# mLSTM units of a one-step diffusion backbone: decay-maximum rows spread by transfers, scaled keys in two buffers, the carried part scaled by ScalarE, PSUM banks laid out anew

## The reference, cut to what matters

```python
b = jnp.cumsum(fb, axis=-1)
log_d = jnp.where(causal, b[..., :, None] - b[..., None, :] + ib[..., None, :], -jnp.inf)
inter = b + m[..., None]
m_t = jnp.maximum(inter, jnp.max(log_d, axis=-1))
s = jnp.einsum('bhtd,bhsd->bhts', qb, kb) * jnp.exp(log_d - m_t[..., None])
w_inter = jnp.exp(inter - m_t)
num = w_inter[..., None] * jnp.einsum('bhtd,bhde->bhte', qb, C) + jnp.einsum('bhts,bhse->bhte', s, vb)
den = w_inter * jnp.einsum('bhtd,bhd->bht', qb, n) + jnp.sum(s, axis=-1)
h = num / jnp.maximum(jnp.abs(den), jnp.exp(-m_t))[..., None]
...
C_new = decay[..., None, None] * C + jnp.einsum('bhs,bhsd,bhse->bhde', w_s, kb, vb)
n_new = decay[..., None] * n + jnp.einsum('bhs,bhsd->bhd', w_s, kb)
```

## Time and profile before

| | us |
|---|---|
| median of 3 runs (lowest, highest) | 2070.65 (2065.98, 2072.45) |
| the profiled execution's own time | 2071.18 |
| its span | 2069.4 |
| PE busy | 1908.4 (92%) |
| DVE busy | 1238.8 (60%) |
| ACT busy | 1086.9 (53%) |
| POOL busy | 706.1 (34%) |

### The profile page before, as it was taken

The page is one execution under the profiler, slowest core; times in us unless marked ns, Lnnn a source line. Parts: engine busy times, 40 slices in busy tenths (PEclk is TensorE's granted clock), DMA queues, the critical chain, the costliest instruction groups (busy, mean ns, idle before and its releaser), DMA issues.

```text
span 2069.4 us, 31383 instructions
## 1 busy us (share of the span) xinstructions
PE 1908.4 (92%) x8796; PEld 1332.9 (64%) x8797; DVE 1238.8 (60%) x1754; ACT 1086.9 (53%) x1548; POOL 706.1 (34%) x738
## 2 busy tenths in 40 slices
PE   8879998999998996799999999999999999999980
PEld 3434445999886454566777767767777777776750
DVE  3575437333777588775666666555566665555646
ACT  5435455342234333565666666666666666665652
POOL 2211000000023044544445534345666653434431
PEclk9999999999999998899999999999999999999995
DMA  8742101342005224347957997866688788886875
GB/s 295 257 143 83 42 21 41 122 123 61 1 1 179 92 92 173 123 158 239 332 169 230 314 343 245 292 186 169 179 263 260 242 272 271 311 296 228 305 198 189
DMA packets 118443, 390.10 MB, mean 189 GB/s; under 512 B 27817, under 2 KB 52461, under 8 KB 93421
## 3 DMA queue, kind: packets, MB, share of 16 engines
q1 hardware_dynamic: 74348, 276.95, 36.2%
q0 software_dynamic: 43744, 112.34, 21.4%
q10 hardware_dynamic: 290, 0.02, 0.0%
HBM read 346.03 MB, written 79.88 MB: 206 GB/s over the span
## 4 chain that ended last, share of the span: by engine, by line
PE 25%; DMA 25%; issue 4%; DVE 3%; ACT 1%; POOL 1%; POOLq 1%; DVEq 0%; ACTq 0%; SPq 0%
DMA yacc_scratch<-y,idx_s 24%; PE bank L1986 14%; PE bank L2009 9%; PE bank L1973 2%; POOL slot_table L1923 1%; DVE wupl L2162 1%; DMA xg<-hn_scratch,idx_g 1%; DVE big L2255 1%; PE bank L1993 1%; DVE xTl L2171 0%; DVE big L2247 0%; DVE y L2246 0%; ACT wuph L2086 0%; DMA shared<-slot_table 0%; DMA y<-yacc_scratch 0%
## 5 line engine op out<-in xcount | busy, mean ns | idle before, releaser
L2162 DVE TENSOR_TENSOR wupl<-big,wuph 128x2048 fp32r<-128x2048 f32 x230 | 517.0, 2289 | 451.0 <-ACT wuph L2086 395.7
L2086 ACT ACTIVATE wuph<-big 128x2048 fp32r (+1 forms) x230 | 428.4, 1916 | 12.5 <-issue 8.5
L2009 PE MATMUL bank<-w,hT 128*128 (+1 forms) x912 | 412.0, 595 | 1.4 <-ACT hT L2071 1.4
L1986 PE MATMUL bank<-wuph,xTh 128*128 128x512 f32 x912 | 367.2, 403 | 12.2 <-DVE xTl L2171 11.9
L1915 POOL DMA_INDIRECT yacc_scratch<-y,idx_s x105 | 220.2, 2097 | 429.4 <-issue 392.8
L1986 PE MATMUL bank<-wuph,xTl 128*128 128x512 f32 x912 | 359.3, 394 | 0.0
L1986 PE MATMUL bank<-wupl,xTh 128*128 128x512 f32 x912 | 358.3, 393 | 0.0
L2009 PEld LDWEIGHTS bank<-w,hT 128*128 128x128 f32 x912 | 165.3, 191 | 166.1 <-issue 166.1
L2076 ACT ACTIVATE y<-bank 128x512 f32<-128x512 f32 x114 | 68.1, 597 | 281.7 <-PE bank L2009 247.6
L1986 PEld LDWEIGHTS bank<-wuph,xTh 128*128 128x128 f32 x912 | 173.4, 190 | 48.5 <-issue 9.7
L1986 PEld LDWEIGHTS bank<-wuph,xTl 128*128 128x128 f32 x912 | 172.2, 189 | 36.7
(11 more groups left out here) (355 smaller groups left out, 2691.9 us busy)
## 6 DMA issues: line engine op xcount, KB each, us to landing
big<-in_exp_w SPq DMA_DIRECT2D x128, 1024.0 KB
w<-in_exp_w SPq DMA_DIRECT2D x64, 1024.0 KB, 7.5
wada<-in_w_ada POOLq DMA_DIRECT2D x16, 1024.0 KB, 6.3
wg<-in_w_in SPq DMA_DIRECT2D x14, 1024.0 KB, 5.3
wada<-in_w_ada SPq DMA_DIRECT2D x4, 2048.0 KB, 19.1
big<-in_w_in SPq DMA_DIRECT2D x8, 1024.0 KB, 5.3
x<-x_scratch SPq DMA_DIRECT2D x9, 512.0 KB
x_scratch<-x SPq DMA_DIRECT2D x9, 512.0 KB, 2.6
```

The costliest lines, as they stand in the source:

```text
L1986: mm = pe.matmul(b_up[j][:, :], x[:, k, :], w[:, :, k, :], start=(k == 0 and i == 0), stop=(k == KT - 1 and i == 2))
L2009: mm = pe.matmul(b_down[half][:, :], hT[:, i, :], w2[:, at, i, half * 512:(half + 1) * 512].rearrange("p s n -> p (s n)"), start=(i == 0), ...
L2086: act.activation(part13(wup[j][0], half), raw13(e % WSLOT, half), ACT.Copy).then_inc(w_high, 1)
L2162: dve.tensor_tensor(part13(wup[j][1], half), raw13(e % WSLOT, half), part13(wup[j][0], half).bitcast(F32), ALU.subtract).then_inc(w_low, 1)
```

## The change

- In the RG-LRU stage SP writes the rows `m.mn` to DRAM once (`mn_rows`). In the mLSTM stage POOL loads, for each unit, the four heads' rows of 128 floats to all 128 partitions (`spread_rows`, 256 KB from repeated rows of 512 bytes), into one of four buffers; the first four before the units, the others four units ahead, behind POOL's inverse root. PE's product L1135 and its bank PM are gone. DVE's L1354 reads the buffer in SBUF and waits for its transfer; the wait for the scores stands before L1359 now.
- `kw` has two buffers, so L1280 of unit n + 1 waits for `products` of unit n - 1.
- The scaling L1365 is done by ACT, behind L1280 of unit n + 1, and signals `carried`. DVE updates S first, then waits for `carried`, then adds; `unit_done` comes after the additions. PE's second half of the first output projection waits for `carried`, since it writes a bank that ACT reads.
- The products of a unit lie in five banks instead of four: those with the state in banks 3 and 4, the weighted scores' in 5 and 6, the increments in 6 and 7.
- Several semaphores are merged (`m.cleared`, `m.squared`, `m.rooted`), with the counts adapted in the other stages.

```diff
             sp.wait_ge(row_d, 4)
             sp.dma_start(o[4][0, 0].rearrange("d h -> h d"), mfin[:, :], allow_slow_non_contiguous=True).then_inc(s_out, 16)
+            sp.wait_ge(row_d, 5)
+            sp.dma_start(m.mn_rows, m.mn).then_inc(m.s_mn, 16)
...
-        kw = work[:, 0:DML].rearrange("p (h e) -> p h e", h=H)
+        kw = [work[:, j * DML:(j + 1) * DML].rearrange("p (h e) -> p h e", h=H) for j in range(2)]
...
-        PS, PM, PX = m.banks[2], m.banks[3], m.banks[4:8]
+        PS, PX = m.banks[2], m.banks[3:8]
...
+        MN_BUFS = 4
+        mn = [m.spare[:, j * DML:(j + 1) * DML].rearrange("p (h t) -> p h t", h=H) for j in range(MN_BUFS)]
+        s_mn = [sem(f"ld_mn{j}") for j in range(MN_BUFS)]
+        rs_ready, carried = sem("root_of_head_ready"), sem("carried_scaled")
...
+        PX_AT = [(2 + h // 3, h % 3) for h in range(H)] + [(h // 3, h % 3) for h in range(H)] + [(3 + h // 2, 1 + h % 2) for h in range(H)]
+
         def px(j):
-            return PX[j // 3][:, (j % 3) * (P + 1):(j % 3 + 1) * (P + 1)]
+            bank, at = PX_AT[j]
+            return PX[bank][:, at * (P + 1):(at + 1) * (P + 1)]
...
-            pool.memset(v[:, :, :, P:P + 1], 1.0).then_inc(pset, 1)
+            pool.memset(v[:, :, :, P:P + 1], 1.0).then_inc(m.cleared, 1)
             pool.wait_ge(w_used, NG)
-            pool.memset(S[:, 0, :, :, :], 0.0).then_inc(pset, 1)
+            pool.memset(S[:, 0, :, :, :], 0.0).then_inc(m.cleared, 1)
             link = Chain(pool, m.pool_steps)
-            for k in range(NT - 1):
+
+            def spread_rows(n):
+
+                d, c, _ = units[n]
+                if n >= MN_BUFS:
+                    pool.wait_ge(logw, n - MN_BUFS + 1)
+                pool.dma_start(mn[n % MN_BUFS], m.mn_rows[:, d, c * P:(c + 1) * P].unsqueeze(0).to_broadcast([P, H, P])).then_inc(s_mn[n % MN_BUFS], 16)
+
+            def root_of_heads(k):
+
                 pool.wait_ge(fin_sq, H * (k + 1))
                 if k >= NFIN:
                     pool.wait_ge(y_ready, k - NFIN + 1)
@@ -1056,6 +1073,15 @@
                 newton_rsqrt_pool(link, pool, v_, r_, rt[:, :], 3)
                 pool.tensor_scalar(r_, r_, 0.5, None, ALU.mult).then_inc(rs_ready, 1)
                 pool.wait_ge(rs_ready, k + 1)
+
+            pool.wait_ge(m.s_mn, 16)
+            for n in range(MN_BUFS):
+                spread_rows(n)
+            for n in range(U):
+                if n - 1 in place:
+                    root_of_heads(place[n - 1])
+                if n + MN_BUFS < U:
+                    spread_rows(n + MN_BUFS)
...
                 if n == -1:
                     pe.wait_ge(free, first)
-                    pe.wait_ge(pset, 2)
+                    pe.wait_ge(m.cleared, 5)
                     pe.wait_ge(s_state, 64)
                 if n + 1 < U:
 
@@ -1131,8 +1157,6 @@
                     ch = slice(c * P, (c + 1) * P)
                     if n >= 0:
                         pe.wait_ge(probs, n + 1)
-                    for h in range(H):
-                        pe.matmul(PM[:, h * P:(h + 1) * P], m.sel[:, h, :], m.mn[:, d, ch], start=True, stop=True)
                     for h in range(H):
                         mm = pe.matmul(PS[:, h * P:(h + 1) * P], kT[:, h, ch], qT[:, h, ch], start=True, stop=True)
                     mm.then_inc(logw_in, 1)
@@ -1152,7 +1176,7 @@
                         pe.matmul(px(h), eb[n % 2][:, h, :], v[:, c, h, :], start=True, stop=True)
                     pe.wait_ge(keys, n + 1)
                     for h in range(H):
-                        mm = pe.matmul(px(8 + h), kw[:, h, :], v[:, c, h, :], start=True, stop=True)
+                        mm = pe.matmul(px(8 + h), kw[n % 2][:, h, :], v[:, c, h, :], start=True, stop=True)
                     mm.then_inc(products, 1)
                 if n == U - 1:
                     pe.wait_ge(probs, U)
@@ -1160,6 +1184,7 @@
                     pe.wait_ge(m.s_wo, 16)
                     mix_half(pe, m, 0, 0)
                 if n == U:
+                    pe.wait_ge(carried, U)
                     mix_half(pe, m, 0, 1).then_inc(m.mixed, 1)
                 if n - 3 in place:
...
                     act.wait_ge(logw, n + 2)
                     act.activation(eb[(n + 1) % 2][:, :, :], eb[(n + 1) % 2][:, :, :], ACT.Exp).then_inc(weights, 1)
                     bank = ring.drain()
-                    if n >= 0:
-                        act.wait_ge(products, n + 1)
+                    if n >= 1:
+                        act.wait_ge(products, n)
                     for h in range(H):
-                        ins = act.activation(kw[:, h, :], bank[:, h * P:(h + 1) * P], ACT.Copy, scale=m.cols[:, j, 1, h:h + 1])
+                        ins = act.activation(kw[(n + 1) % 2][:, h, :], bank[:, h * P:(h + 1) * P], ACT.Copy, scale=m.cols[:, j, 1, h:h + 1])
                     ring.drained(ins)
                     act.wait_ge(free, ring.n)
                     act.sem_inc(keys, 1)
+                if 0 <= n < U:
+                    d, c, _ = units[n]
+                    j = d * NT + c
+                    act.wait_ge(products, n + 1)
+                    if n >= 1:
+                        act.wait_ge(h_new, n)
+                    for h in range(H):
+                        ins = act.activation(nd[:, h, :], px(4 + h), ACT.Copy, scale=m.cols[:, j, 2, h:h + 1])
+                    ins.then_inc(carried, 1)
...
-                    dve.wait_ge(logw_in, n + 2)
+                    e = eb[(n + 1) % 2]
+                    dve.wait_ge(s_mn[(n + 1) % MN_BUFS], 16 * ((n + 1) // MN_BUFS + 1))
                     if n >= 1:
                         dve.wait_ge(products, n)
                     for h in range(H):
-                        ins = dve.scalar_tensor_tensor(eb[(n + 1) % 2][:, h, :], PM[:, h * P:(h + 1) * P],
-                                                       m.cols[:, j, 0, h:h + 1], m.neg[d], ALU.add, ALU.add)
+                        ins = dve.scalar_tensor_tensor(e[:, h, :], mn[(n + 1) % MN_BUFS][:, h, :], m.cols[:, j, 0, h:h + 1], m.neg[d], ALU.add, ALU.add)
                     ins.then_inc(logw, 1)
                     dve.wait_ge(weights, n + 2)
-                    e = eb[(n + 1) % 2]
+                    dve.wait_ge(logw_in, n + 2)
                     dve.tensor_tensor(e[:, :, :], e[:, :, :], PS[:, :].rearrange("p (h t) -> p h t", h=H), ALU.mult).then_inc(probs, 1)
                 if 0 <= n < U:
                     d, c, second = units[n]
                     seq, j = min(c, 1), d * NT + c
                     dve.wait_ge(products, n + 1)
                     for h in range(H):
-                        ins = dve.tensor_scalar(nd[:, h, :], px(4 + h), m.cols[:, j, 2, h:h + 1], None, ALU.mult)
+                        st = S[:, seq, d, h, :]
+                        ins = dve.scalar_tensor_tensor(st, st, m.decb[:, h, d, c:c + 1], px(8 + h), ALU.mult, ALU.add)
                     link(ins)
+                    dve.wait_ge(carried, n + 1)
                     for h in range(H):
                         ins = dve.tensor_tensor(nd[:, h, :], nd[:, h, :], px(h), ALU.add)
-                    link(ins)
-                    for h in range(H):
-                        st = S[:, seq, d, h, :]
-                        ins = dve.scalar_tensor_tensor(st, st, m.decb[:, h, d, c:c + 1], px(8 + h), ALU.mult, ALU.add)
                     ins.then_inc(unit_done, 1)
```

More of the change, by code:

```diff
@@ L241, in stage_norm1 @@
             "mod_summed1", "mod_row", "mod_columns_in", "mod_columns_ready", "gate_sums"))
-        x_pos, x_sq, x_root, x_hn = (sem(n) for n in ("x_pos", "x_sq", "x_root", "x_hn"))
+        x_pos, x_hn = (sem(n) for n in ("x_pos", "x_hn"))
         done_act, done_dve = sem("modulated_act"), sem("modulated_dve")
@@ L268, in _ @@
                 if g == 0:
-                    sp.wait_ge(bd_zero, 1)
+                    sp.wait_ge(m.cleared, 1)
                     for d in range(2):
@@ L388, in root @@
                 if t >= 1:
-                    act.wait_ge(x_sq, t)
-                act.activation(sq, x[t][:, :], ACT.Square, accum_out=ss[:, t:t + 1]).then_inc(x_sq, 1)
-                act.wait_ge(x_sq, t + 1)
-                act.activation(rs[:, t:t + 1], ss[:, t:t + 1], ACT.Sqrt, scale=1.0 / D, bias=m.epsc).then_inc(x_root, 1)
+                    act.wait_ge(m.squared, t)
+                act.activation(sq, x[t][:, :], ACT.Square, accum_out=ss[:, t:t + 1]).then_inc(m.squared, 1)
+                act.wait_ge(m.squared, t + 1)
+                act.activation(rs[:, t:t + 1], ss[:, t:t + 1], ACT.Sqrt, scale=1.0 / D, bias=m.epsc).then_inc(m.rooted, 1)
             def mod_copies(j):
@@ L450, in norm @@
             def norm(t):
-                dve.wait_ge(x_root, t + 1)
+                dve.wait_ge(m.rooted, t + 1)
                 link(dve.reciprocal(rs[:, t:t + 1], rs[:, t:t + 1]))
@@ L561, in _ @@
         def _(pool):
-            pool.memset(xrp[:, :], 0.0).then_inc(zeroed, 1)
```

(29 more changed lines are left out.)

16 lines of the change are left out of this document (8 added, 8 removed).

## The result

| | before | changed | ratio (95% interval) |
|---|---|---|---|
| first comparison, 4 and 4 runs | 2071.22 (2065.98 to 2072.45) | 2049.04 (2046.46 to 2053.72) | 0.9893 (0.9874 to 0.9912) |
| second comparison, 11 and 6 runs | 2072.55 (2068.12 to 2078.54) | 2045.84 (2040.84 to 2053.69) | 0.9878 (0.9858 to 0.9898) |

Times in us, medians with lowest and highest. The change wins about 1.1%, 22 us in the first comparison. The profiled execution after took 2053.72 us (span 2051.9), the second one that was profiled 2040.84 us (span 2039.1).

A forecast was written before the change was run, and what follows sets the result against it. PE's own work was taken to bound early units (8.75 us), a chain of waits across engines the late ones (10.3). Savings of 1.0, 13.7, 5.1 and 1.5 made 21.3 us: 2071.2 - 21.3 = 2049.9, range 2045 to 2060.

The forecast's parts named there:

- The likeliest case: Whole kernel: all the expected savings arrive and later stages move forward unchanged, 2049.9 us; chance 0.70.
- iterations 0 to 13: mLSTM units: 115.24 us becomes 9 x 7.74 + 3 x 7.9 + 8.2 = 101.6, 13.7 less.
- iterations 13 to 16: Late mLSTM units, where PE also turns finished rows: 30.9 us becomes 3 x 8.6 = 25.8, 5.1 less.
- to the output projection: From the last unit's scores to L1405, the output projection: 13.08 us becomes 11.57, 1.5 less.
- Step 1: Early units, bound by PE: removing L1135 saves 1.0 us (bounds 0.88 and 1.09), period 7.74 us.
- more is won: Rival, chance 0.10: clock stays up in the last unit (1.7 us) and L1135's whole 1.09 goes; 2047 us.
- Step 2: Late units: a chain across DVE and ACT, with two `kw`, sets 8.6 us; half gate still waits for L1280.
- the light cases: Iterations 2, 11, 12 (second unit divided, no gate applied yet) take 7.9 us; iteration 4, bound by PE, 8.2.
- the late units keep their period: Rival, chance 0.12: ACT needs twice as long for the carried part, chain 9.75 us, kernel 2059 us.
- Step 3: Last unit: L1149 comes 7.15 us behind the scores, 4.42 more to L1405 at the lower clock; 11.57 instead of 13.08.
- Step 4: Costs put at nothing: 18 row transfers, at most 5.2 us each, issued four units ahead; DVE's SBUF operand changes nothing.
- What would show it: Signs: no L1135, early units 7.7 us, late 8.6, DVE waiting for `carried`, L1405 near 634 us, later distances unchanged.

The follow-up runs named there:

- dve_scales: The changed kernel with DVE scaling the carried part again, behind its update of S; ratio to the kernel before 0.9910, units' stage 169.49 us.
- one_kw: The changed kernel with one key buffer `kw` instead of two; ratio to the kernel before 0.9926, units' stage 172.13 us.
- carried_more: The changed kernel with ACT scaling six pieces instead of four, the extra two into unused space; one run 2046.06 us, units' stage 168.90 us.
- rows_only: The changed kernel with one `kw` and DVE scaling the carried part, keeping spread rows and new banks; ratio to the kernel before 0.9920, stage 169.57 us.

## Why the prediction was right, point by point

**The time.** 2049.9 was forecast, 2049.04 and 2045.84 measured, both in the range. The likeliest case held: less work for PE in the early units, a shorter cross chain in the late ones, and nothing given back up to the end of the routing stage. The sum of 21.3 us stands against 21.6 in the stage, but its terms were off in both directions, so that it comes within 0.3 us is luck; so is a whole time within 1 us, since the two profiled executions of the changed kernel lie 12.9 us apart. The terms:

| term | predicted | measured |
|---|---|---|
| iteration -1 to 0 | 1.0 | 1.27 |
| iterations 0 to 13 | 13.7 | 16.4 |
| iterations 13 to 16 | 5.1 | 4.0 |
| to the output projection | 1.5 | 0.26 |
| from there to the routing stage | 0 | -0.39 |

The remaining 0.1 us is in the first half gate.

**Step 1, mis-sized.** The mechanism was right: PE is full, DVE is not late, and the period falls by L1135. Its price was 1.28 us, outside the bounds of 0.88 and 1.09. I read it as the distance from L1135 to L1137, but the distances on both sides of the group were 0.1 us longer each, which the one distance does not hold. The rival "more is won" was right on this half (it would have L1135's whole 1.09) and wrong on the other, the clock.

**Step 2, the chain right, the light cases wrong.** The steady late units take 8.75 us, 8.6 was forecast (the terms listed there add up to 8.56, not 8.54). In the trace after, one such unit on DVE and ACT (start, duration, idle before):

```profile
606.20 1.12 ACT L1305 ACTIVATE big<-bank,cols 128x128 f32<-128x128 f32 x4
607.49 1.14 ACT L1316 ACTIVATE big<-bank,cols 128x129 f32<-128x129 f32 x4 [0.17 <-ACT big L1305]
608.74 0.88 DVE L1404 TENSOR_TENSOR big<-big,bank 128x129 f32<-128x129 f32 x4 [0.69 <-ACT big L1316]
...
613.24 1.14 DVE L1389 SCALAR_TENSOR_TENSOR eb<-shared,cols,cst 128x128 f32<-128x128 f32 x4
```

ACT's scaling takes 1.14 where 1.15 was taken, it starts 0.17 us behind the keys where 0.06 was taken, and DVE waits 0.69 us for it. The step that failed is the sentence "The half gate of the next iteration still waits for L1280", where I applied it to every unit. It waits for the keys only behind turned rows. So the light iterations 2, 11 and 12 do not take 7.9 but PE's 7.46, and what DVE and ACT fall behind in them is paid in one piece, by the first unit with turned rows: 9.27 us in iteration 4 (8.2 forecast) and 9.42 in iteration 13 (8.6). The rival "the late units keep their period" is out: ACT's price is not doubled. But `dve_scales`, `one_kw` and `carried_more` show how near it was: a little more lateness costs a second time through the clock.

**Step 3, mis-sized.** `unit_done` came 7.50 us behind the last scores (7.15 forecast) after an idle time of 2.89. The clock went down as forecast, but stayed down longer: the three product groups took 5.32 us from there to L1437 where 4.42 was taken from the earlier trace rows, and the first projection half 7.42 against 7.13. Of the 1.5 us hoped for, 0.26 came.

**Step 4, right.** No L1389 but the first waits for its rows, and that one ahead of the first scores. A transfer landed in 4.0 us (median), 7.5 at most, above the 5.2 that I had estimated as the most but well inside the lead. POOL spends 0.77 us on each issue, hidden. The page "DMA: Bandwidth & Descriptors" of the Trainium skill, section "Anatomy of one DMA", gives a formula by which I estimated 2.6 us; the trace has half as much again. DVE's adds from SBUF take 347 ns each (L1389), those with the PSUM operand took 343 at the median (L1354 before); unchanged was forecast, and the wide pairs of the earlier trace rows say the same, and the lower fixed term from SBUF in the table of "VectorE: DVE Perf Modes" of the Trainium skill, section "The TRN2 errata", is not to be seen. That section of the Trainium skill adds that its VectorE row comes out too low against a measurement from SBUF.

**What would show it.** No L1135, PE full in the early units, DVE waiting for `carried`, L1437 at 632.50 (634 forecast): all there. "Everything behind it at its old distance" holds to the end of the routing stage. Behind that the two profiled executions of the same kernel differ by 12.5 us. From 780 us on PE is busy equally long within 1.6 us (1169.35 and 1167.83). Of the difference, 7.6 us lie ahead of PE's last instruction, and there its waits for DVE differ most. From 780 us to the end (in total, times, longest) they are in the one

```profile
PE bank L2018 <- DVE xTl L2203: 14.2, 15, 4.9
```

and in the second

```profile
PE bank L2018 <- DVE xTl L2203: 9.5, 10, 4.9
```

The other 5.0 us lie behind it, where the last results are scattered and added up. What makes the difference was not tried. It is the reason why a single execution says little about 3 us of this kernel.

## What to carry to other kernels

When engines share a ring of buffers in order, write down which earlier fill each fill waits for before you price a chain: a wait that shows in some units may be absent in the others, and the lateness that gathers there is paid at once when the order shifts. An edit that shortens a gap can be worth more than the time it takes off the gap if TensorE's clock stays up by it (0.76 us less of a gap, and 1.7 us less of a half gate). Moving ready work into a gap keeps the clock there, but look behind the stage as well: the work is then missing where it stood, and the clock fell at the next gaps instead (2.3 of 2.6 us given back). The price of a group of small products is found by adding or removing the group; the distance to the next group alone came out 0.19 us short here.

## What the hardware showed that I had not expected

- Four float32 products with four weight rows cost 1.28 us between groups of full weights, and four with 128 weight rows 0.89 us, beside the same scores and with the same 128 columns: the smaller product was the dearer one.
- TensorE ran slower behind short gaps. After idle times of 0.86 and then 2.02 us a half gate took 5.41 us instead of 3.62; after 0.47 and 2.02, 5.11; after 2.02 with no idle time recorded before L1194, 5.37; after 1.61 (`rows_only`, iteration 4) and after 1.26, 3.72. After 2.89 us three product groups ran at half speed (1.93 to 2.09 us each instead of 1.06). After 2.02 and then 1.50 us, 16 passes of 512 columns took 9.25 us instead of 6.94 (granted clock 0.75 instead of 1.00).
- A transfer of 256 KB from repeated rows of 512 bytes, issued by POOL, took 3.6 us at least, 4.0 in the middle and 7.5 at most from issue to landing.
